# A two-block transformer step on one core: seven query chunks of the second block rotated through transfers and GpSimd, and index scores weighed by ScalarE

## The reference, cut to what matters

```python
def _rope(x, pos):
    d = x.shape[-1]
    half = d // 2
    inv_freq = ROPE_THETA_2 ** (-(jnp.arange(half, dtype=jnp.float32) * 2.0 / d))
    ang = pos.astype(jnp.float32)[..., None] * inv_freq
    cos = jnp.cos(ang)[:, :, None, :]
    sin = jnp.sin(ang)[:, :, None, :]
    xf = x.astype(jnp.float32)
    x1, x2 = xf[..., :half], xf[..., half:]
    out = jnp.concatenate([x1 * cos - x2 * sin, x2 * cos + x1 * sin], axis=-1)
    return out.astype(x.dtype)
...
    q = _rope(_rmsnorm(q, q_norm_g), positions)
...
        s = jnp.einsum('bqhd,bsd->bqhs', qib, ki)
        score = jnp.einsum('bqhs,bqh->bqs', jax.nn.relu(s), wib).astype(jnp.float32)
        causal = key_idx[None, :] <= t_idx[:, None]
        score = jnp.where(causal[None], score, -jnp.inf)
        _, sel = lax.top_k(score, topk)
```

## Time and profile before

| | before |
|---|---|
| median of 3 runs | 1758.34 us (1758.05 to 1759.43) |
| profiled execution | 1755.06 us |
| its span | 1753.3 us |
| TensorE matmul busy | 1676.4 us (96%) |
| VectorE busy | 1027.1 us (59%) |
| ScalarE busy | 703.2 us (40%) |
| GpSimd busy | 65.0 us (4%) |
| mean granted TensorE clock | 0.983 |

### The profile page before, as it was taken

The page is one execution under the profiler, slowest core; times in us unless marked ns, Lnnn a source line. Parts: engine busy times, 40 slices in busy tenths (PEclk is TensorE's granted clock), DMA queues, the critical chain, the costliest instruction groups (busy, mean ns, idle before and its releaser), DMA issues.

```text
span 1753.3 us, 23024 instructions
## 1 busy us (share of the span) xinstructions
PE 1676.4 (96%) x7756; PEld 1335.0 (76%) x7756; DVE 1027.1 (59%) x2032; ACT 703.2 (40%) x1331; POOL 65.0 (4%) x46
## 2 busy tenths in 40 slices
PE   6998999999998999889999999999999899999999
PEld 5777677777886766557788888887888788888887
DVE  7788766666456698944755553466454533333334
ACT  5364666662344234763333322224223333332322
POOL 0020000000000063000000000000000000000000
PEclk9999999999998998999999999999999999999999
DMA  6453344444321121002355554352323233333323
GB/s 238 156 156 112 141 137 156 144 145 150 96 93 54 46 63 47 1 13 85 123 193 194 193 207 133 108 191 87 97 94 100 69 108 96 96 96 97 96 96 108
DMA packets 56455, 202.30 MB, mean 115 GB/s; under 512 B 6512, under 2 KB 6640, under 8 KB 56240
## 3 DMA queue, kind: packets, MB, share of 16 engines
q1 hardware_dynamic: 56368, 201.16, 34.8%
HBM read 198.38 MB, written 2.10 MB: 114 GB/s over the span
## 4 chain that ended last, share of the span: by engine, by line
PE 86%; DVE 9%; ACT 3%; issue 2%; DMA 0%; DVEq 0%; ACTq 0%
PE bank L469 24%; PE bank L471 24%; PE bank L470 24%; PE bank L571 2%; PE bank L621 2%; PE bank L512 1%; PE bank L513 1%; DVE WORK L1919 1%; PE bank L592 1%; DVE W_lo L1397 1%; DVE SM L1918 1%; PE bank L515 1%; PE bank L518 1%; PE bank L527 1%; PE bank L707 0%
## 5 line engine op out<-in xcount | busy, mean ns | idle before, releaser
L469 PE MATMUL bank<-H_hi,W_hi 128*128 128x512 f32 x1336 | 533.3, 399 | 4.4 <-DVE W_lo L1397 3.3
L471 PE MATMUL bank<-H_hi,W_lo 128*128 128x512 f32 x1336 | 520.5, 390 | 0.0
L470 PE MATMUL bank<-H_lo,W_hi 128*128 128x512 f32 x1336 | 520.5, 390 | 0.0
L1397 DVE TENSOR_TENSOR W_lo<-RAW,W_hi 128x512 fp32r<-128x512 f32 x538 | 351.9, 693 | 197.0 <-ACT W_hi L895 182.8
L895 ACT ACTIVATE W_hi<-RAW 128x512 fp32r<-128x512 f32 x538 | 317.1, 625 | 273.5 <-PE bank L471 224.2
L469 PEld LDWEIGHTS bank<-H_hi,W_hi 128*128 128x128 f32 x1336 | 250.8, 188 | 74.6 <-issue 19.5
L470 PEld LDWEIGHTS bank<-H_lo,W_hi 128*128 128x128 f32 x1336 | 250.9, 188 | 54.2 <-issue 4.5
L471 PEld LDWEIGHTS bank<-H_hi,W_lo 128*128 128x128 f32 x1336 | 250.8, 188 | 53.5
L469 PE MATMUL bank<-A_hi,W_hi 128*128 128x512 f32 x352 | 136.9, 389 | 0.0
L470 PE MATMUL bank<-A_lo,W_hi 128*128 128x512 f32 x352 | 136.9, 389 | 0.0
L471 PE MATMUL bank<-A_hi,W_lo 128*128 128x512 f32 x352 | 136.9, 389 | 0.0
(11 more groups left out here) (262 smaller groups left out, 2020.9 us busy)
## 6 DMA issues: line engine op xcount, KB each, us to landing
RAW<-weights SPq DMA_DIRECT2D x269, 512.0 KB, 3.7
AW<-ada SPq DMA_DIRECT2D x100, 512.0 KB, 3.7
X<-x_t SPq DMA_DIRECT2D x4, 512.0 KB, 6.2
y_t<-X SPq DMA_DIRECT2D x8, 256.0 KB, 2.0
LW<-lru_w SPq DMA_DIRECT2D x1, 1024.0 KB, 12.2
QX<-QR SPq DMA_DIRECT2D x40, 16.0 KB
CROW<-crow SPq DMA_DIRECT2D x1, 512.0 KB, 10.2
ROPE<-rope SPq DMA_DIRECT2D x1, 512.0 KB, 13.0
```

Of the source, the lines that this page charges most:

```text
L469: pe.matmul(dst, wh, ch(hi, k), start=(k == 0), stop=False)
L470: pe.matmul(dst, wh, ch(lo, k), start=False, stop=False)
L471: mm = pe.matmul(dst, wl, ch(hi, k), start=False, stop=(k == chunks - 1))
L1397: dve.tensor_tensor(W_lo[:, w], RAW[:, c:c + HALF], W_hi[:, w], ALU.subtract).then_inc(lo_done, 1)
```

## The change

Chunks i = 6 to 12 lose their `rot2` matmul and VectorE's product with the sine. Instead SyncE exchanges the halves with four transfers of 32 rows from `QN` to a new buffer `QX2` (`query_halves`), placed in front of the weight load of steps `T_QKV2` + 10 to + 16; GpSimd multiplies by the sine (`times_sine`), one chunk behind its cosine product; VectorE only adds (`query_turned`). The add of chunk i now stands in VectorE's loop c = i + 5, where it was c = i + 4, and that of chunk 12 stands after the second score of step 17. Chunk 13 keeps its matmul. The weight products of the index heads of block 3 move from GpSimd to ScalarE (`weighed`), after the two `relu`s and ahead of `head_out`. `QN` and `QR` get other places in their rings.

```diff
--- before.py
+++ after.py
@@ -277,6 +277,7 @@
         SQ = at("SQ", 2 * S, unit[7] + S * 24)
         QR = at("QR", 3 * S, unit[4])
         QN = at("QN", 3 * S, unit[4] + S * 12)
+        QX2 = at("QX2", 2 * S, unit[4] + S * 24)
         RAB = at("RAB", 2 * S, unit[6])
         SS = at("SS", S, unit[7] + S * 20)
         ssg = cursor[0]
@@ -330,7 +331,8 @@
             "kcol_mm", "krinv", "krow_mm", "krow_used", "k_sum", "kd_done"))
         qcol_mm = sem("qcol_mm")
         head_var, head_pow = sem("head_var"), sem("head_pow")
-        q_cos, sum_step = sem("q_cos"), sem("sum_step")
+        q_cos, q_sin, sum_step, relu_scaled = sem("q_cos"), sem("q_sin"), sem("sum_step"), sem("relu_scaled")
+        q_half = [sem("q_half0"), sem("q_half1")]
         wi_mm, wi_done = sem("wi_mm"), sem("wi_done")
         xc_done, xsq_done = sem("xc_done"), sem("xsq_done")
         idx_mm, relu_done, relu_used = sem("idx_mm"), sem("relu_done"), sem("relu_used")
@@ -420,7 +422,19 @@
                     for a, b in ((head, head + 8), (head + 8, head)):
                         sp.dma_start(QX1[c % 3][a:a + 8, :], ch(QR1, c % 3)[b:b + 8, :]).then_inc(half_in[c % 3], 16)
 
+            def query_halves(i):
+
+                sp.wait_ge(head_in, i + 1)
+                if i >= 8:
+                    sp.wait_ge(rope_done, 10 + i - 1)
+                for head in (0, HD):
+                    for to, rows in ((head, head + HD // 2), (head + HD // 2, head)):
+                        sp.dma_start(QX2[to:to + HD // 2, (i % 2) * S:(i % 2 + 1) * S],
+                                     ch(QN, (i + 2) % 3)[rows:rows + HD // 2, :]).then_inc(q_half[i % 2], 16)
+
             for t in range(0, T_FFN0):
+                if T_QKV2 + 10 <= t <= T_QKV2 + 16:
+                    query_halves(t - T_QKV2 - 4)
                 if T_Q < t <= T_Q + 10:
                     swap_halves(t - T_Q - 1)
                 raw(Tile(t + 4))
@@ -703,8 +717,8 @@
             def rot2(i):
 
                 pe.wait_ge(head_in, i + 1)
-                pe.wait_ge(rope_done, 10 + i)
-                pe.matmul(ps[3][:], cs("rot2"), ch(QN, (i + 1) % 3), start=True, stop=True).then_inc(rot_mm, 1)
+                pe.wait_ge(rope_done, 10 + min(i, 6))
+                pe.matmul(ps[3][:], cs("rot2"), ch(QN, (i + 2) % 3), start=True, stop=True).then_inc(rot_mm, 1)
 
             def index(n, k):
 
@@ -789,11 +803,10 @@
                     if c:
                         if k == 2:
                             query_columns(c - 1)
-                        if k == 3:
-                            rot2(6 + c - 1)
                     if c == 7 and k == 5:
                         pe.wait_ge(kd_done, 2)
                         pe.wait_ge(relu_done, IDX_UNITS)
+                        pe.wait_ge(rope_done, 10 + 10)
                         qk(16, (0, 1, 2))
                 return body
 
@@ -1195,9 +1208,9 @@
                 if i >= 3:
                     act.wait_ge(rope_done, 10 + i - 2)
                 if gain is None:
-                    ins = act.copy(ch(QN, (i + 1) % 3), ps[tile.bank][:])
+                    ins = act.copy(ch(QN, (i + 2) % 3), ps[tile.bank][:])
                 else:
-                    ins = act.mul(ch(QN, (i + 1) % 3), ps[tile.bank][:], pr(gain))
+                    ins = act.mul(ch(QN, (i + 2) % 3), ps[tile.bank][:], pr(gain))
                 ins.then_inc(head_in, 1)
                 if i == 13:
                     act.activation(ch(SQ, q % 2), ps[tile.bank][:], ACT.Square).then_inc(head_sq, 1)
@@ -1213,6 +1226,18 @@
                 w = S if u < 4 else (3 * P if u < 12 else S)
                 act.activation(RL[:, (u % NRL) * S:(u % NRL) * S + w], ps[(5, 7)[u % 2]][:, 0:w],
                                ACT.Relu).then_inc(relu_done, 1)
+
+            def weighed(u):
+
+                h = u - 12
+                rl, wcol = RL[:, (u % NRL) * S:(u % NRL + 1) * S], WI[:, 24 + h:25 + h]
+                act.wait_ge(relu_done, u + 1)
+                if h == 0:
+                    act.wait_ge(relu_used, u)
+                    act.mul(SCALL[:, 2 * S:3 * S], rl, wcol).then_inc(relu_used, 1)
+                    act.sem_inc(relu_scaled, 1)
+                else:
+                    act.mul(rl, rl, wcol).then_inc(relu_scaled, 1)
 
             split_hi(Tile(T_QKV2 + 2), (1,))
             index_keys_out()
@@ -1244,6 +1269,8 @@
                 if c < 13:
                     relu(12 + 2 * (c - 9))
                     relu(13 + 2 * (c - 9))
+                    weighed(12 + 2 * (c - 9))
+                    weighed(13 + 2 * (c - 9))
                 head_out(c, c - 3, "q_g")
             exps(16)
             for s in range(16, 32):
@@ -1343,25 +1370,24 @@
 
             def index_sum(h):
 
-                u, w = 12 + h, S
+                u = 12 + h
                 dst = SCALL[:, 2 * S:3 * S]
-                pool.wait_ge(relu_done, u + 1)
-                rl, wcol = RL[:, (u % NRL) * S:(u % NRL) * S + w], WI[:, 24 + h:25 + h]
-                if h == 0:
-                    pool.tensor_scalar(dst, rl, wcol, None, ALU.mult).then_inc(relu_used, 1)
-                else:
-                    pool.tensor_scalar(rl, rl, wcol, None, ALU.mult).then_inc(sum_step, 1)
-                    pool.wait_ge(sum_step, h)
-                    pool.wait_ge(relu_used, u)
-                    pool.tensor_tensor(dst, dst, rl, ALU.add).then_inc(relu_used, 1)
+                pool.wait_ge(relu_scaled, h + 1)
+                pool.wait_ge(relu_used, u)
+                pool.tensor_tensor(dst, dst, RL[:, (u % NRL) * S:(u % NRL + 1) * S], ALU.add).then_inc(relu_used, 1)
                 if h == 7:
                     pool.wait_ge(relu_used, u + 1)
-                    pool.tensor_tensor(dst[:, w - P:w], dst[:, w - P:w], cs("mask_diag"), ALU.add).then_inc(sum_step, 1)
+                    pool.tensor_tensor(dst[:, 3 * P:], dst[:, 3 * P:], cs("mask_diag"), ALU.add).then_inc(sum_step, 1)
 
             def times_cosine(i):
                 pool.wait_ge(head_in, i + 1)
-                pool.wait_ge(rope_done, 10 + i - 1)
-                pool.tensor_tensor(ch(QR, i % 2), ch(QN, (i + 1) % 3), ROPE[:, 0:S], ALU.mult).then_inc(q_cos, 1)
+                pool.wait_ge(rope_done, max(10 + i - 2, 16))
+                pool.tensor_tensor(ch(QR, (i + 1) % 3), ch(QN, (i + 2) % 3), ROPE[:, 0:S], ALU.mult).then_inc(q_cos, 1)
+
+            def times_sine(i):
+                pool.wait_ge(q_half[i % 2], 64 * ((i - 6) // 2 + 1))
+                pool.wait_ge(rope_done, max(10 + i - 1, 16))
+                pool.tensor_tensor(ch(RAB, 1 - i % 2), ch(QX2, i % 2), ROPE[:, S:2 * S], ALU.mult).then_inc(q_sin, 1)
 
             power(0)
             power(1)
@@ -1370,12 +1396,13 @@
             for i in range(6, 14):
                 if i in (11, 13):
                     power(3 if i == 11 else 4)
-                if i >= 10:
-                    times_cosine(i)
+                if 6 < i < 10:
+                    index_sum(2 * (i - 6))
+                times_cosine(i)
                 if i < 10:
-                    index_sum(2 * (i - 6))
-                    times_cosine(i)
                     index_sum(2 * (i - 6) + 1)
+                if i > 6:
+                    times_sine(i - 1)
             power(5)
 
 
@@ -1848,14 +1875,22 @@
                 link(dve.tensor_tensor(b, rotated, ROPE[:, S:2 * S], ALU.mult))
                 if src is None:
                     dve.wait_ge(q_cos, i - 5)
-                    a = ch(QR, i % 2)
+                    a = ch(QR, (i + 1) % 3)
                 if dst is not None:
                     link(dve.tensor_tensor(dst, a, b, ALU.add))
 
+            def query_turned(i):
+
+                dve.wait_ge(q_cos, i - 5)
+                dve.wait_ge(q_sin, i - 5)
+                dve.tensor_tensor(ch(Q, i - 6), ch(QR, (i + 1) % 3), ch(RAB, 1 - i % 2), ALU.add).then_inc(rope_done, 1)
+
             def rope2_out(i):
-                dve.wait_ge(rot_mm, i + 1)
+                if i == 13:
+                    dve.wait_ge(rope_done, 10 + i)
+                dve.wait_ge(rot_mm, min(i, 6) + 1)
                 dst = ch(QI, i) if i < 4 else (ch(QR, i - 4) if i < 6 else ch(Q, i - 6))
-                turned(i, ch(QN, (i + 1) % 3) if i < 6 else None, ps[3][:], dst)
+                turned(i, ch(QN, (i + 2) % 3) if i < 6 else None, ps[3][:], dst)
                 dve.sem_inc(rope_done, 1)
 
             def index_keys_normed():
@@ -1914,7 +1949,7 @@
                     w = (n + 1) * P
                     score, work = SCALL[:, (n - 1) * S:(n - 1) * S + w], WORK[:, 0:w]
                     if q == 0 and n == 3:
-                        dve.wait_ge(sum_step, 8)
+                        dve.wait_ge(sum_step, 1)
                     link(dve.max(M8, score if q == 0 else work))
                     link(dve.match_replace(work, M8, score if q == 0 else work, TAKEN))
                     if q == TOPK // 8 - 1:
@@ -1984,7 +2019,8 @@
                     query_variance(0)
```

(4 more changed lines are left out.)

## The result

The changed kernel takes 1763.69 us in the median of 11 runs (1759.02 to 1764.3), the kernel before 1758.34 in 11 (1755.54 to 1760.62): ratio 1.0023, 95% interval 1.0014 to 1.0032. By the ratio it is slower by 0.23%, by the two medians by 0.3% (5.35 us), and 1763.69 lies outside the range of the prediction (1754.8 to 1761.3). The profiled execution has 1759.26 us and a span of 1757.3, 4.0 us over that of before.

A forecast was written before the change was run, and what follows sets the result against it. VectorE's list was taken to set when attention starts; its 3.0 us gain, spent waiting for GpSimd behind the last tile, left 0.5 us at the third score: 1758.34 - 0.5 = 1757.8 us, range 1754.8 to 1761.3.

The forecast's parts named there:

- VectorE sets the pace, TensorE's 6 us do not arrive.: Query tiles: TensorE loses seven `rot2`, 6.0 us, the most that could be won; VectorE's list sets when attention starts.
- c = 10 and c = 11.: VectorE's loops: most of c = 10's 1.85 us goes idle, c = 11's add waits 1.5; gain so far 0.3.
- the line on c = 13: VectorE's loop c = 13: GpSimd's products end at 654.35, VectorE comes at 654.0; gain 2.4 us.
- "Gain 3.0" at c = 15.: VectorE's loop c = 15: VectorE comes at 668.2, waits 1.3 us for GpSimd's products until 669.55; gain 3.0.
- a rival: Tiles 13 to 16: GpSimd and VectorE hold each other up, 7 us less 0.5, about 1764.8 us; chance 0.12.
- "VectorE's 3 us arrive at the first score and are spent waiting for GpSimd.": Behind the last tile: variance to third score takes 9.2 us, before 6.7; third score at 684.4 against 684.96.
- The transfers.: SyncE: exchanged halves 6.0 us after `QN`, nothing waits; rival of late transfers, some 35 us at worst, chance 0.04.
- The clock.: First attention steps: 5 us more or less at the low level, up to 2 us either way; chance 0.06.
- "past 700 us": Sign that the prediction is wrong: TensorE's low clock lasts past 700 us.

The follow-up runs named there:

- the sine on VectorE: Changed kernel with the sine product back on VectorE, from the halves that the transfers bring; GpSimd has only cosine products: ratio to before 1.0001.
- the power behind the products: Changed kernel with GpSimd's 24-column power behind the cosine product of chunk 13 and sine product of chunk 12, not ahead: ratio to before 1.0021.
- chunk 12 by matmul: Changed kernel with chunk 12 rotated by matmul and VectorE's sine product again, in the loop of c = 16: ratio to before 1.0019.
- the sine product first: Changed kernel with GpSimd's sine product of chunk i - 1 ahead of power, index sum and cosine product of chunk i; transfers' wait changed: ratio 1.0001.
- the held kernel: Changed kernel with GpSimd's products held back until VectorE has split and added, powers, first variance and second root step moved: ratio 0.9973, 1752.91 us.
- the same places without the transfers: Kernel before with weights on ScalarE and the held kernel's places for powers, variance and roots, all chunks by matmul: ratio 1.0029.

## Why the prediction was wrong

- *VectorE sets the pace, TensorE's 6 us do not arrive.* Right: the sine on VectorE shows it, and TensorE stalled 0.53 us before tile 14 and 0.37 before tile 16 on `W_lo`, where I had put tiles 15 and 16. Its `rot2(13)` was slow in some runs and was waited for there, but behind the last tile.
- *c = 10 and c = 11.* Right in kind. VectorE idled 1.14 us for `W_hi` and then 1.23 for the sine product (I said 1.5). The rounds of c = 11 started 0.3 us later than before, not 0.3 earlier: the pair of splits took 2.67, and the index sum and the sine product that the add waited for took 1.73 and 1.72, not 1.28. In the line on c = 13 the terms add up to 654.2, not 654.35; nothing hangs on it.
- *"Gain 3.0" at c = 15.* **This is the step that failed.** The gain up to c = 14 was 2.6 us (3.3 said), and c = 15 took 2.3 of it, not 0.3: splits +1.1 us, the add +1.0, and the sine product ready 1.8 us later than said, as the variance came later (0.8) and the power (5.80 us, not 5.45), cosine and sine products took 1.0 more. The second variance came 0.30 us early, not 3.0. I had the mechanism in a rival and dismissed it with "there its products lie beside selection rounds". But my own sum had `power(3)` push `times_cosine(11)` and `times_sine(10)` to 667.0 to 669.55, and VectorE at its add at 668.2, so that its pair of splits (1.29 us) ran from 666.9: the two overlap in my own numbers. The sum priced that overlap at nothing. That rival's price for a full collision, 1.4 us a loop, was short: a pair of splits and an add together lost 2.1 in c = 15.
- *"VectorE's 3 us arrive at the first score and are spent waiting for GpSimd."* Right as a mechanism: 9.7 us from the variance to the third score (9.2 said, 6.7 before), 3.68 us of idle (about 3 said). With 3.0 in and 2.5 out the sum was -0.5; with 0.3 in and 3.0 out it was +2.7 at the third score. The 0.5 us more behind the last tile is the power (4.53 us, not 4.15) and what lay around it. Taking this list away did not bring the time back (the power behind the products, and chunk 12 by matmul): TensorE's slow `rot2(13)` and new collisions stood behind it, and the forecast has neither.
- *The transfers.* Right: they landed 2.0 us after their issue in the median (3.7 at most), and neither GpSimd nor VectorE waited for one in the changed kernel. Where the sine product came earlier on GpSimd's list, GpSimd did wait for them: six times, 8.8 us in all, with the sine product first.
- *The clock.* I gave it 0.06 and called it a case of its own. It was no rival but a term: the low level began 3.2 us earlier and ended 7.0 later than before, and one attention step more ran in it, 0.83 us. It ended at 701.5 us, so my sign for it ("past 700 us") did show. The prediction tied it to TensorE's longer idle time. The runs don't bear that out for the fall (it came as early behind 1.15 us of idle in the held kernel); why it rose late, at 85.0 and not 78.0, stays open.

## What to carry to other kernels

Price work that goes to GpSimd twice: its own time on the list, and up to 1.1 us for each two-operand SBUF instruction of VectorE that it meets; then lay both lists side by side in time before believing that they miss each other. Place it beside instructions that it doesn't stretch (here MAX8 and MATCH_REPLACE8), by order or by a wait. And when one limit is taken away, look at which level the clock has where the next one stands: a pair of matmuls that took 1.1 us just before the clock fell took 2.07 just after, and in four of these kernels it was the next thing waited for.

## What the runs showed of the hardware

- When a VectorE instruction with two SBUF operands met a GpSimd product or sum of 128x512, the one that started later was held. In the 13 kernels VectorE's splits and adds of 128x512 took over 0.80 us, not 0.69, 80 times in the query tiles and just behind them; 76 of them ended 0.53 to 0.57 us after the end of a GpSimd tensor_tensor that had started first (the other four met a TENSOR_SCALAR). So adds of 0.69 us took up to 1.82, and pairs of 1.29 up to 3.21. Where VectorE was first, GpSimd's product or sum ended 1.1 to 1.2 us after VectorE's instruction (67 of 69). Both directions, from the changed kernel and from the one with the same places without the transfers:

```profile
671.65 1.28 POOL L1385 TENSOR_TENSOR QR<-QN,ROPE 128x512 f32<-128x512 f32 x1
671.80 1.68 DVE L1886 TENSOR_TENSOR Q<-QR,RAB 128x512 f32<-128x512 f32 x1 [1.25 <-POOL RAB L1390]
...
675.40 0.69 DVE L1862 TENSOR_TENSOR Q<-QR,RAB 128x512 f32<-128x512 f32 x1
675.47 1.76 POOL L1372 TENSOR_TENSOR QR<-QN,ROPE 128x512 f32<-128x512 f32 x1 [5.96 <-ACT QN L1200]
```

- MAX8 and MATCH_REPLACE8 (0.55 us at 384 columns) were never stretched. The Trainium skill says of the shared interfaces (GPSIMD Engine Reference, Key points) that the contention is with VectorE instructions "in a 2-port perf mode or with two SBUF inputs"; the traces agree for the second, with these numbers. The first of the two may be behind the TENSOR_SCALAR on 128x32 that took 1.25 us instead of 0.18 beside the cosine product in the last kernel; no run here tests it.
- Even tiny ones are caught. In the held kernel root steps of 128x32 elements took 1.26 and 1.21 us, not 0.19, beside the products of chunk 12. The loss goes with what is left of GpSimd's product, not with the size of VectorE's instruction.
- The powers held nobody up. In the kernel before, VectorE's add at 664.50 took its 0.69 us in the middle of the power of 5.45 (663.95), and in the changed kernel the root steps at 679.04 and after took 0.18 to 0.21 beside the power of 4.53. In the 13 kernels no VectorE split or add that met only a power took over 0.70 us (36 of them).
- GpSimd's power of 32 columns took 5.43 to 5.83 us, one of 24 columns 4.15 to 4.60, one of 8 columns 1.63 to 1.82.
- TensorE's granted clock fell to 0.50 between 64.2 and 71.0 us from tile 9 in every kernel, where the tiles end and the first attention steps begin, behind idle times from 0.33 to 6.05 us, and stayed there for 6.8 to 24 us (10.3 before, 20.5 in the changed kernel, 13.7 in the held one). In every kernel it fell again later in the attention, for 3.4 to 6.8 us at a time; with the sine product first that was at 132.7 us for 6.8 us, and the projection came 3.9 us later than the third score says. What decides the length is open.
